# A two-block transformer kernel: attention scores of the second block as fp32r products of high and low parts stacked over 128 rows, in place of native fp32 products over 64 rows

## The reference, cut to what matters

```python
z = h @ w_in[l]                     # queries, keys, values of all branches, gates
o_nsa  = _nsa(...)                  # 8 heads of 64, 2 key groups
o_ret  = _retention(q_r, k_r, ...)  # 4 heads, rotated queries and keys of 64
o_conv = _conv_module(c_a, c_b)     # depthwise convolution of width 31
...
s_c = einsum('bqghd,bngd->bghqn', qb, k_cmp)   # queries x 15 compressed keys
s_s, s_w = ...                                 # queries x 256 selected / window keys
inner = einsum('bnchd,bnehd->bnhce', qc, kc)   # retention scores
```

## Time and profile before

| | |
|---|---|
| median of 3 runs | 2553.78 us (2547.5 to 2557.94) |
| the profiled execution | 2547.57 us, span of the trace 2545.8 us |
| PE busy | 2475.4 us, 97% of the span |
| DVE busy | 1980.2 us, 78% |
| ACT busy | 1457.8 us, 57% |
| mean granted TensorE clock | 0.983 of full speed |

### The profile page before, as it was taken

How to read it: one execution, slowest core, us unless ns; L and a number is a source line. 1 busy time by engine, 2 the same in 40 slices (tenths; PEclk the granted TensorE clock), 3 DMA queues, 4 the chain that set the end, 5 groups by cost and what they waited for, 6 DMA issues and landing times.

```text
span 2545.8 us, 30098 instructions
## 1 busy us (share of the span) xinstructions
PE 2475.4 (97%) x11752; PEld 2033.6 (80%) x11752; DVE 1980.2 (78%) x2461; ACT 1457.8 (57%) x1472; POOL 32.3 (1%) x44
## 2 busy tenths in 40 slices
PE   8999988999999999999999997999999999999998
PEld 6678877788888888888888886877778878777887
DVE  5855567989898989898989887779775566896655
ACT  4344442777777777777777674455444544544543
POOL 0000000000000000000000000000000000000000
PEclk9999998999999999999999998999999998999999
DMA  8356544799999999999999996443555563344564
GB/s 268 107 183 190 175 156 168 273 352 362 354 362 352 362 353 360 355 361 354 362 343 369 346 367 223 148 145 108 165 182 183 182 217 126 109 148 157 190 190 133
DMA packets 274157, 626.20 MB, mean 246 GB/s; under 512 B 17899, under 2 KB 27255, under 8 KB 273880
## 3 DMA queue, kind: packets, MB, share of 16 engines
q1 hardware_dynamic: 271708, 615.92, 69.8%
q0 software_dynamic: 1872, 6.82, 0.8%
q10 hardware_dynamic: 428, 1.45, 0.1%
HBM read 623.06 MB, written 1.07 MB: 245 GB/s over the span
## 4 chain that ended last, share of the span: by engine, by line
PE 88%; DVE 10%; ACT 1%; issue 1%; DMA 0%; POOL 0%; DVEq 0%; SPq 0%; POOLq 0%; ACTq 0%
PE tile L644 26%; PE tile L646 26%; PE tile L645 25%; PE aux L764 4%; DVE units_parts L1772 2%; PE aux L1012 1%; DVE zbuf L2366 1%; PE aux L1192 1%; PE aux L1128 1%; PE aux L1213 1%; ACT high L1338 0%; DVE acts L1728 0%; DVE x_sb L1859 0%; DVE acc L1897 0%; ACT acts L1368 0%
## 5 line engine op out<-in xcount | busy, mean ns | idle before, releaser
L1772 DVE TENSOR_TENSOR units_parts<-units,high 128x1024 fp32r<-128x1024 f32 (+3 forms) x514 | 727.7, 1423 | 320.5 <-ACT high L1338 314.4
L1338 ACT ACTIVATE high<-units 128x1024 fp32r<-128x1024 f32 (+3 forms) x514 | 624.6, 1218 | 484.5 <-PE tile L646 443.5
L644 PE MATMUL tile<-high,acts 128*128 128x512 f32 (+2 forms) x1688 | 668.9, 396 | 16.7 <-DVE units_parts L1772 9.7
L645 PE MATMUL tile<-units_parts,acts 128*128 128x512 f32 (+2 forms) x1760 | 681.8, 387 | 0.0
L646 PE MATMUL tile<-high,acts 128*128 128x512 f32 (+2 forms) x1688 | 654.9, 388 | 0.0
L644 PEld LDWEIGHTS tile<-high,acts 128*128 128x128 f32 x1688 | 322.3, 191 | 85.8 <-DVE units_parts L1772 21.0
L645 PEld LDWEIGHTS tile<-units_parts,acts 128*128 128x128 f32 x1760 | 336.1, 191 | 62.3 <-issue 0.5
L646 PEld LDWEIGHTS tile<-high,acts 128*128 128x128 f32 x1688 | 321.4, 190 | 65.2
L646 PE MATMUL tile<-high,zbuf_parts 128*128 128x512 f32 x692 | 269.7, 390 | 0.0
L645 PE MATMUL tile<-units_parts,zbuf_parts 128*128 128x512 f32 x632 | 245.9, 389 | 0.0
L644 PE MATMUL tile<-high,zbuf_parts 128*128 128x512 f32 x596 | 234.3, 393 | 0.0
(11 more groups left out here) (334 smaller groups left out, 3537.6 us busy)
## 6 DMA issues: line engine op xcount, KB each, us to landing
units<-in_moe_w SPq DMA_DIRECT2D x216, 1024.0 KB, 5.3
units<-in_w_in SPq DMA_DIRECT2D x136, 512.0 KB, 3.6
units<-in_w_ff SPq DMA_DIRECT2D x128, 512.0 KB, 3.5
q_buf<-in_moe_w SPq DMA_DIRECT2D x54, 1024.0 KB, 5.4
k_buf<-in_moe_w SPq DMA_DIRECT2D x54, 1024.0 KB, 5.4
nat<-in_moe_w SPq DMA_DIRECT2D x54, 1024.0 KB, 5.2
units<-in_ffn_w SPq DMA_DIRECT2D x62, 512.0 KB, 3.8
units<-in_w_out SPq DMA_DIRECT2D x32, 512.0 KB, 3.3
```

The costliest lines, as they stand in the source:

```text
L644: nc.tensor.matmul(bank, lhs[0], high, start=start, stop=False)
L645: nc.tensor.matmul(bank, lhs[0], low, start=False, stop=False)
L1338: nc.scalar.activation(high_slot(SG[0], n) if wide_ else high_slot(SG[0], n)[:, 0:cols], halves(weights) if wide_ else weights[:, 0:cols], ...
L1772: V.tensor_tensor(low, weights, high, ALU.subtract).then_inc(SG[0].low_ready, 1)
```

## The change

The four `q` banks of a layer are now read twice: ScalarE writes the rounded high part to 64 rows (`high_of`), VectorE the low part to the other 64 rows (`low_of`, bank minus high). The keys' high part is written by ScalarE to both halves of the rows (`k_twice`), and VectorE writes their low part to a third place (`k_low`). `kcmp` gets high twice, low once and a column of zeros. A score is then two fp32r products: the stacked query parts over 128 rows times the twice stored high keys, and the high queries over 64 rows times the low keys. The retention's rotated heads move from `q_buf` to `acc`, heads 0 and 1 in rows 0 to 63 and heads 2 and 3 in rows 64 to 127; its products stay native fp32, and ScalarE begins to read them once all four transposed banks are full.

```diff
-            kcmp = sb("kcmp", [64, 2, N_CMP], where=two)
+            kcmp = sb("kcmp", [P, 2, 2, N_CMP + 1], F32R, where=two)
...
-        rot_t = q_buf[64:128, :].rearrange("p (h t) -> p h t", h=8)
+        q_s = q_parts[:, :].rearrange("p (h t) -> p h t", h=8)
+        k_twice, k_low = k_parts[:, 0:1024], k_parts[0:64, 1024:2048]
+        k_twice, k_low = (v.rearrange("p (g t) -> p g t", g=4) for v in (k_twice, k_low))
+        rot_t = acc[:, 1, :].rearrange("p (c t) -> p c t", t=SEQ)
...
+                def score_parts(dst, h, b, keys_twice, keys_low):
+                    both = q_s[:, h, b * P:(b + 1) * P]
+                    nc.tensor.matmul(dst, both, keys_twice, start=True, stop=False)
+                    return nc.tensor.matmul(dst, both[0:64, :], keys_low, start=False, stop=True)
...
-                        at = (b * NSA_H + h) * N_CMP
-                        mm = nc.tensor.matmul(bank[:, at:at + N_CMP], q_t[:, h, b * P:(b + 1) * P],
-                                              kcmp[:, h // 4, :], start=True, stop=True)
+                        at = (b * NSA_H + h) * (N_CMP + 1)
+                        mm = score_parts(bank[:, at:at + N_CMP + 1], h, b, kcmp[:, 0, h // 4, :],
+                                         kcmp[0:64, 1, h // 4, :])
...
-                    nc.tensor.matmul(aux_bank()[:, 0:2 * nk].rearrange("p (r k) -> p r k", r=2),
-                                     q_t[:, h, b * P:(b + 1) * P], k_t[:, g:g + 3:2, 0:nk],
-                                     start=True, stop=True).then_inc(S2.aux_full, 1)
+                    mm = score_parts(aux_bank()[:, 0:2 * nk].rearrange("p (r k) -> p r k", r=2), h, b,
+                                     k_twice[:, g:g + 3:2, 0:nk], k_low[:, g:g + 3:2, 0:nk])
+                    mm.then_inc(S2.aux_full, 1)
...
-                turn_in(k_t[:, 0:4, b * P:(b + 1) * P], turned_at["k", l] + b)
+                    for half in (64, 0):
+                        high_of(k_twice[half:half + 64, :, b * P:(b + 1) * P], turned_at["k", l] + b)
...
                     if u == ROTATED_AT:
+                        act.wait_ge(S2.aux_full, turned_at["rot", l] + 2 * TB)
...
-                C.aux.take(2)
-                bank = aux_in()
-                evac(V.tensor_copy(kcmp[:, :, :], bank[0:64, 0:2 * N_CMP].rearrange("p (g n) -> p g n", g=2)))
+
+                def query_lows(b):
+                    for h in range(2):
+                        low_of([q_s[half:half + 64, 4 * h:4 * h + 4, b * P:(b + 1) * P] for half in (0, 64)])
+
+                query_lows(0)
+                keys = aux_in()[0:64, 0:2 * N_CMP].rearrange("p (g n) -> p g n", g=2)
+                high, low = (kcmp[0:64, i, :, 0:N_CMP] for i in range(2))
+                V.memset(kcmp[:, :, :, N_CMP:N_CMP + 1].bitcast(F32), 0.0)
+                V.tensor_copy(kcmp[64:128, 0, :, 0:N_CMP], keys)
+                step(V.tensor_copy(high, keys))
+                evac(V.tensor_tensor(low, keys, high, ALU.subtract))
...
                 fill()
-                C.aux.take(2)
+                query_lows(1)
                 fill()
                 taps_on(TAPS_SCORES)
...
                 V.tensor_tensor(s2, s2, spread(small[:, 0:16], N_CMP), ALU.mult).then_inc(cmp_probs, 1)
+                for b in range(TB):
+                    C.turned.take()
+                    low_of([v[0:64, :, b * P:(b + 1) * P] for v in (k_twice, k_low)])
                 fill()
```

More of the change, by code:

```diff
@@ L1243, in _ @@
                             for h in range(2):
-                                turn([rot[:, b, 4 * h + i, :] for i in range(4)])
+                                turn([rot[:, b, 2 * h + i, :] for i in (0, 1, 4, 5)])
                         turned_rot = C.aux.n
@@ L1258, in ret_scores @@
                     bank = aux_bank()
-                    nc.tensor.matmul(bank[:, 0:SEQ], rot_t[:, 4 + h, 0:P], rot_t[:, h, 0:SEQ], start=True, stop=True)
-                    nc.tensor.matmul(bank[:, SEQ:SEQ + P], rot_t[:, 4 + h, P:SEQ], rot_t[:, h, P:SEQ],
+                    q, k = (rot_t[64 * (h // 2):64 * (h // 2) + 64, 2 * i + h % 2, :] for i in range(2))
+                    nc.tensor.matmul(bank[:, 0:SEQ], k[:, 0:P], q, start=True, stop=True)
+                    nc.tensor.matmul(bank[:, SEQ:SEQ + P], k[:, P:SEQ], q[:, P:SEQ],
                                      start=True, stop=True).then_inc(S2.aux_full, 1)
@@ L1570, in _ @@
                     for h in range(2):
-                        turn_in(q_t[:, 4 * h:4 * h + 4, b * P:(b + 1) * P], turned_at["q", l, b] + h)
+                        high_of(q_s[0:64, 4 * h:4 * h + 4, b * P:(b + 1) * P], turned_at["q", l, b] + h)
                     later.go_on(next(fills))
@@ L1589, in _ @@
                     if u == ROTATED_AT:
+                        act.wait_ge(S2.aux_full, turned_at["rot", l] + 2 * TB)
                         for b in range(TB):
                             for h in range(2):
-                                turn_in(rot_t[:, 4 * h:4 * h + 4, b * P:(b + 1) * P], turned_at["rot", l] + 2 * b + h)
+                                turn_in(rot_t[64 * h:64 * h + 64, :, b * P:(b + 1) * P],
+                                        turned_at["rot", l] + 2 * b + h)
                     if u == NSA_AT:
@@ L2417, in _ @@
                 for b in range(TB):
-                    n = NSA_H * N_CMP
+                    n = NSA_H * (N_CMP + 1)
                     c0 = (TB - b) * P - P + CMP_BLOCK - 1
```

## The result

| kernel | median us | lowest to highest | runs |
|---|---|---|---|
| before | 2551.59 | 2547.50 to 2560.57 | 20 |
| changed | 2563.90 | 2558.31 to 2571.23 | 20 |

The account below looks back on a forecast made before the run. The prediction took TensorE to bound the loop over heads up to u = 13 and VectorE behind it. Its terms summed to +2.4 - 3.1 + 0.7 = 0.0 us a layer, giving 2554 us, range 2546 to 2563.

Parts of the forecast that it names:

- wait for the query lows: Ahead of the compressed scores: TensorE stands still until VectorE has written the queries' low parts, +1.7 us a layer.
- 32 compressed records: The compressed scores' 32 short products, now alternating between 128 and 64 rows: +0.4 us a layer.
- wait for the key lows: Ahead of the loop's first scores: TensorE waits for two key lows behind VectorE's probabilities, +1.1 us a layer.
- scores 0 to 2: Scores ahead of u = 1, where TensorE is the bound: they save 0.6 to 1.2 us, taken as -0.8 a layer.
- clock elsewhere: Behind the compressed scores: the low clock begins earlier or lasts longer, +0.7 us a layer, bounds 0 and +3.
- u = 1 to 13: Iterations of the loop over heads: faster TensorE brings VectorE forward by 3.1 us a layer, bounds 0 and 5.9.
- Bounds 0 and +0.9: Limits, in us a layer, for the extra cost of the 32 compressed records, from which +0.4 was taken.
- the prediction's own signs of being wrong: No TensorE wait ahead of compressed scores, shorter VectorE stretch behind u = 13, 32 products over 5 us, low clock over 8.
- the sum's own worst case, +13: Both layers with every term at its worst bound: 13 us slower; the best case was -9.
- the slower one: Rival: standing still and bare loads pull the clock down in the compressed scores; chance 0.10 whole, 0.17 half.
- The whole of it: Slower rival in full: 0.33 us a compressed record, +7 to +9 us a layer, 2568 to 2571 us; chance 0.10.
- the half of it: Half of the slower rival's clock and load loss at the compressed scores: +5 to +10 us over two layers; chance 0.17.

Follow-up runs that it names:

- The repeat: The changed kernel run once more, unchanged; median 2563.01 us, 1.0046 of the kernel before.
- e1: Changed kernel with zeros under the low compressed keys, so the compressed scores' second products run over 128 rows; 2556.69 us, 1.0028 of the kernel before.
- e2: Changed kernel with the two products of every second compressed score in the other order, halving the changes of height; 2561.43 us, 1.0041 of the kernel before.
- e8: Changed kernel with zeros under the low keys of the loop alone, compressed scores still alternating in height; 2557.30 us, 1.0021 of the kernel before.
- e10: Kernel before with the copies of `kcmp` and `vcmp` two fills later, so TensorE waits ahead of the compressed scores; 2559.38 us, 1.0028 of the kernel before.
- e5: As e7, with eight convolution taps moved from steps u = 8 to 15 to the last two fills ahead of the loop; 2540.79 us, 0.9960 of the kernel before.
- e11: As e5, with the second half's query lows also ahead of the split of a weight unit; 2540.24 us, 0.9949 of the kernel before.
- e7: Changed kernel with all scores padded to 128 rows and the second half's query lows ahead of three taps; 2546.71 us, 0.9981 of the kernel before.

## Why the prediction was wrong

The terms a layer, predicted and read from the profiled execution of the changed kernel:

| term | predicted | layer 0 | layer 1 |
|---|---|---|---|
| wait for the query lows | +1.7 | +2.2 | +2.2 |
| 32 compressed records | +0.4 | +6.0 | +5.1 |
| wait for the key lows | +1.1 | +1.55 | +1.9 |
| scores 0 to 2 | -0.8 | +0.2 | +0.2 |
| clock elsewhere | +0.7 | +1.4 | +1.5 |
| u = 1 to 13 | -3.1 | -3.7 | -3.7 |
| sum | 0.0 | +7.7 | +7.2 |

Scores 0 to 2 are read as the first four records, 1.22 us against 1.06; the clock elsewhere as u = 0, 5.18 against 3.75, in which score 2 lies. Together 14.9 us; the two profiled executions differ by 19.85, of which 4.8 had arisen at 1651 already, before the changed code began (read at ScalarE's copies of weight units, which are the same in both), and the medians differ by 12.3. That 14.9 and 4.8 come so near to 19.85 is in part luck, since two stretches that nearly cancel stand in no row: in layer 1 the clock fell once more behind scores 0 and 1 (12.91 us from them to score 2, against 11.30), and behind layer 1's loop, near 2298 us, it fell in the kernel before and not in the changed one, where the distance shrinks by some 1.5. The repeat's profiled execution, 2559.31 us, lies 11.7 above that of before, 1.6 of them from ahead of 1651.

**The step that failed** is the one on the compressed scores, with its "Bounds 0 and +0.9" and its "+0.4". The bounds came from rows in which every product had the height of the one before, though the text had just said that the new ones alternate, and had read 0.09 us for a load of 64 rows behind one of 128. Taken at its word, that row gives 32 x 0.09 = 2.9 us a layer on top, twice 2.9 = 5.8 in all, without any clock: the forecast would have been 2560. e1, e2 and e8 show that this price is real, 0.09 to 0.10 a change. The clock does the rest: 0.31 - 0.205 = 0.105 for each record that runs at the low level, some 3 us a layer. So the +0.4 measured 6.0 and 5.1. Two of the prediction's own signs of being wrong came with it: the 32 products took more than 5 us, and the low clock, counted from their start, lasted some 17 us in layer 0 and 20 in layer 1, over the 8 allowed. The term for the clock behind them, "+0.7", was too small by the same fall: u = 0 alone lost 1.4 and 1.5 us. And the median lies inside the sum's own worst case, +13; the range of 2546 to 2563 had been drawn narrower than the bounds of its terms.

**The rival that came closest** was the slower one: 0.33 a record, decided by "the clock is low at the first of the 32 records". Measured were 0.31, with the clock low from record 3 on in layer 0 and from the first in layer 1. The whole of it, 2568 to 2571, was 4 to 7 us too dear; the half of it, +5 to +10, ended at 2564, where the median lies, though the 12.3 us to the kernel before are more than that half. The two had a chance of 0.27 together. What spoke against it, that layer 0 of the kernel before ran its 32 records at 0.117, was read from records of one height that TensorE reached without standing still.

**The loads.** The 0.09 us were in the rows and are now measured by e1 and e2. The Trainium skill, "TensorE: Matmul & The Clock Gate", section "Step-by-step: what each phase is for", ties the pull-ahead of a load to row groups that don't conflict or to the background buffer; the prediction named it and put no price of its own on it. It agrees with the alternating records, whose loads of 0.18 to 0.19 us lie bare, one behind the other. It does not by itself tell why 128 rows behind 128, which share all row groups, cost nothing extra (0.11, e1), unless through the buffer. The same section says that for the time of a load the row count doesn't matter; here the count as such doesn't (0.18 us for 64 rows, 0.19 for 128), but its change decides whether the load is hidden.

**Right, by their own steps.** Both waits of TensorE appeared where they were put, released by the low parts named, each 0.45 to 0.8 us longer than forecast. The loop's gain was 3.7 for 3.1, and it came where it was put: 1.05 up to u = 6 (forecast 1.0), 1.6 up to u = 7 (1.6), 2.1 behind it (1.3 to 1.8), by VectorE's reads at 1704.67, 1725.09, 1730.88 and 1759.81; VectorE's waits fell to 2.7, most of it at u = 6 to 7; from u = 13 the chain is VectorE's for 38 us, as before. A score step of 0.52 and 0.75 is above the 0.24 to 0.44 and 0.46 to 0.66 of the forecast: native 0.63 and 1.05 were read a little high (0.71, 1.14), and each border costs 0.09 to 0.2 and not at worst 0.1. Up to u = 8, where TensorE still bounds the loop, it hardly counted, since what padding could win there before VectorE's bound was 0.9 us (e8); behind u = 8 VectorE's bound hid it.

**A term of the wrong sign.** The "-0.8" for scores 0, 1 and 2, from "0.6 to 1.2", was wrong in sign: four records of alternating height in a row save nothing over native ones of one height. With both heights equal they take 0.55 (e8).

## What to carry to other kernels

Stacking high and low parts over 128 rows leaves a second product over 64; before counting its columns, count how often the height of consecutive products changes, and where many tiny ones stand together pad the short ones with zeros, since of 16 columns a product over 128 rows behind one over 128 costs 0.11 us and one over 64 behind it 0.205. Where a saving on TensorE doesn't come through, find who reads its result next: here VectorE took all but a quarter of what padding saved in the loop, and most of the gain came with moving its work out of the loop, 2540.8 us against 2551.8 (0.996, 0.9946 to 0.9974), where the padded kernel had 2546.7 without the move (0.9981) and the same move alone brought 2.3. And a wait placed ahead of a run of tiny products was lost whole (e10); that it costs a second time through the clock behind it was so in one layer of e10 (2.8 us) and not in the other.

## What the runs showed of the hardware

- A change of height between consecutive products costs 0.09 to 0.10 us at either clock: 0.205 against 0.112 a step at the full one, 0.310 against 0.213 at half (16 columns). With 256 columns in the loop the first product's step is 0.21 against 0.11, and the second's, followed by transposes of 128 rows, 0.31 against 0.12; that the way back to 128 rows costs twice as much there was not explained.
- An fp32r product of 16 columns over 128 rows takes the same 0.112 us as one of the two records of a native fp32 product of 15 columns over 64: with so few columns the parts save nothing.
- The clock's fall in one and the same kernel came at different records in the two layers and in two executions (2 and 0, 6 and 13 of 32), after the same wait. What decides stays open. e5 and e11 kept the full clock in all four stretches, though in three of them it fell within 1.3 us behind; e7, which differs from e5 by the place of eight taps alone, in neither of its two.
